# GpSimd's subtraction of a weight chunk in pieces of 256 columns, in a two-block transformer kernel

## The chip, the cores and the metric

The kernel runs on one core of one Trainium2 chip. The metric is the device time of one execution in microseconds (us). The engines are named as in the profile: PE is TensorE (PEld its weight loads), DVE is VectorE, ACT is ScalarE, POOL is GpSimd, SP is SyncE, which here only issues DMAs. An SP, ACT or POOL queue works strictly in order, and so does DVE's.

## The reference

Batch 1, 512 tokens, 1024 channels, all fp32. Two blocks follow each other. Cut to its big matrix products, the reference is:

```python
# first block, layer 0: gated MLP with a spatial unit, and a multiscale pool
h = x * (1 + scale) + shift                        # shift, scale, gate = silu(c) @ ada_w[l] + ada_b[l]
u, v, z_a, x_b, z_b = split(h @ e_w_in, 5)         # 1024 x 5120
a = u * (W_s @ layer_norm(v) + b) * silu(z_a)
b = (pool(x_b) @ pool_w + pool_b) * pool_scale * silu(z_b)
x = layer_norm(ALPHA * x + (1 + gate) * (concat(a, b) @ e_w_out))
# layer 1: latent attention, 16 heads
q_c, kv_c, k_r, z = split(h @ o_w_in); q = rms(q_c) @ w_uq; ...
x = layer_norm(ALPHA * x + (1 + gate) * ((attention * silu(z)) @ o_w_out))
# second block: short convolution, feed-forward, windowed attention, feed-forward
h = h + rmsnorm((b_gate * conv3(c_gate * u)) @ a_w_out)
h = h + rmsnorm((silu(g) * up) @ w_down)           # g, up = rmsnorm(h) @ w_gate_up, 1024 x 5632
h = h + rmsnorm(window_attention(...) @ b_w_o)
h = h + rmsnorm((silu(g) * up) @ w_down)
```

## The kernel before

**Split products.** Each fp32 operand of a large product is held as two tiles of a narrower fp32 format: a high part, which is a rounded copy, and a low part, which is the fp32 value minus the high part. A product is then three matmuls (`mm3`, lines 1589 to 1591): high by high, high by low, low by high.

**Weights.** All weights pass through a ring of two slots `s` = 0, 1. A chunk is 128 partitions by 2048 columns (`CHUNK`; 1280 for one slot of the latent attention). It goes through four stations: SP loads it into `w_raw[s]` (`load`, line 402); ACT copies it into `w_high[s]` (`split_high`, line 655); GpSimd forms `w_low[s]` = `w_raw[s]` - `w_high[s]` (`low`, line 589); PE reads high and low. The semaphores between them are `w_full`, `w_high`, `w_split` and `used`. When GpSimd is done, it frees `w_raw[s]` for the next load (`raw_free`). So with two slots, while PE works through one chunk of 48 matmuls of 512 columns, the other slot is freed by PE, copied by ACT and subtracted by GpSimd. A few chunks are split by DVE instead (`split_low`, line 1204), and the second chunk of the stages gu0, kv and gu1 is shared in halves (line 598 on GpSimd, 1212 on DVE).

**Stages**, in the order of the table `RING`: v, xb, zu, pool, zb, eout (layer 0), lat, mla (eight rounds of two heads), oout (layer 1), cu, b, aout (convolution), gu0, dn0 (feed-forward), kv, q, wo (windowed attention), gu1, dn1 (feed-forward).

**Other work on DVE.** DVE evacuates PSUM, does the normalisations, the softmax parts and the low parts of the activations. In stages xb, zu and zb it also multiplies and reduces the conditioning weights `ada_w`: two multiplications `gains<-gains,csil` of 1024 columns (line 1033, both inputs in SBUF) and two reductions to `ada_acc` (line 1036), whose results PE needs after each chunk (line 1636), and whose end lets SP load the next piece. The gated stages form `gate_buf` times PSUM (1159, 1163), times `sv` (1165), and the low part `mix_low` or `ff_low` (1168), the last two with both inputs in SBUF.

**Other work on GpSimd.** `pool_low` (line 626, 4096 columns, one instruction), eight passes over `x` by the layer norm's gain and bias (582, 584), and parts of the rotary of the windowed attention (571, 574). Every operation of an engine's program is in source order; there is no scheduler.

Of the kernel before, what the change touches and what calls it, by code (L numbers as in the profile page):

```python
# [6 lines left out]
F32 = mybir.dt.float32  # L7
F32R = mybir.dt.float32r
I32 = mybir.dt.int32
ALU = mybir.AluOpType  # L10
# [170 lines left out]


UNITS = KVH * T
CREDIT = 1


def program(nc, a, out):
    with ExitStack() as ctx:

        def sem(name):  # L190
            return ctx.enter_context(nc.semaphore(name))
# [6 lines left out]
        def at(name, offset, shape, dt=F32):  # L198
            return nc.alloc_sbuf_tensor_at(name, shape, dt, offset=start + offset)

        raw = [at(f"w_raw{s}", 8 * KB * s, [P, CHUNK]) for s in range(2)]
        WH = [at(f"w_high{s}", (16 + 8 * s) * KB, [P, CHUNK], F32R) for s in range(2)]
        WL = [at(f"w_low{s}", (32 + 8 * s) * KB, [P, CHUNK], F32R) for s in range(2)]
# [119 lines left out]
        w_split = [sem(f"w_split{s}") for s in range(2)]  # L323
# [37 lines left out]

        PF, n = {}, CREDIT
        for name in ("xb", "zu", "zb", "cu", "b", "gu0", "gu1"):
# [3 lines left out]
        SG, n = {}, 0  # L367
# [24 lines left out]
        def _(sp):  # L392
# [4 lines left out]
            def load(name, i, s, pieces):  # L397
                B = BASE[name]
                assert len(pieces) == B.dmas[s]
                sp.wait_ge(raw_free[s], B.use[s] + i + CREDIT)  # L400
                for dst, src in pieces:
                    sp.dma_start(dst, src).then_inc(w_full[s], 16)
# [9 lines left out]
            def deep(s, w, kt, n=2):  # L412
                c = n * D // 2
                return [(raw[s][:, j * c:(j + 1) * c], w[:, kt + j, :] if n == 2 else w[:, kt, j * c:(j + 1) * c]) for j in range(2)]
# [20 lines left out]
            def ada_load(layer, pos, first):  # L435

                for m in range(2):
                    sp.wait_ge(ada_sum[m], pos + CREDIT)
                    sp.dma_start(ada_buf[m], ada_w[layer][:, :, bass.ds(pos * 256 + (first + m * P), P)]).then_inc(ada_land[m], 16)
# [50 lines left out]
            for s in range(2):  # L490
                load("oout", 0, s, deep(s, w_in["o_w_out"], s * 2))
            sp.wait_ge(oz_ready, HEADS + CREDIT)
            for j, src in ((1, a["ln_g"][1:2, :]), (2, a["ln_b"][1:2, :]), (3, a["a_pre"])):
# [60 lines left out]
        @block.gpsimd  # L554
        def _(pool):
            nc.gpsimd.memset(eps[:, 0:1], LN_EPS)
            nc.gpsimd.memset(eps[:, 1:2], EPS2).then_inc(pool_ready, 1)
            for s in range(2):
                pool.sem_inc(raw_free[s], CREDIT)
                pool.sem_inc(pair_free[s], CREDIT)  # L560
            pool.sem_inc(gate_low, 2)
            pool.sem_inc(oz_ready, CREDIT)
            pool.sem_inc(sz_ready, CREDIT)
            for m in range(2):
                pool.sem_inc(ada_sum[m], CREDIT)

            def turn_queries(g):

                dst = q2[g % 2][:, :, :]
                pool.wait_ge(q2_raw, g + 1)  # L570
                nc.gpsimd.tensor_tensor(dst, q2raw[:, :, :], cosB.unsqueeze(1).broadcast_to((P, 2, S)), ALU.mult).then_inc(q2_cos, 1)
                pool.wait_ge(q2_cos, g)
                pool.wait_ge(q2_sin, g)
                nc.gpsimd.tensor_tensor(dst, dst, q2tmp[:, :, :], ALU.add).then_inc(q2_ready, 1)

            for name, pairs, _ in RING:
                B = BASE[name]
                if name == "mla":
                    pool.wait_ge(gains_in, 32)
                    for t in range(T):  # L580
                        pool.wait_ge(tr_done, T * TR["eout"] + t + 1)
                        nc.gpsimd.tensor_tensor(x[:, t, :], x[:, t, :], gains[:, 1, :], ALU.mult).then_inc(pool_step, 1)
                        pool.wait_ge(pool_step, t + 1)
                        nc.gpsimd.tensor_tensor(x[:, t, :], x[:, t, :], gains[:, 2, :], ALU.add).then_inc(x_ready, 1)

                def low(i, s, n=CHUNK):

                    pool.wait_ge(w_high[s], B.split[s] + i + 1)
                    nc.gpsimd.tensor_tensor(WL[s][:, 0:n], raw[s][:, 0:n], WH[s][:, 0:n].bitcast(F32), ALU.subtract).then_inc(w_split[s], 1)  # L589
                    pool.wait_ge(w_split[s], B.split[s] + i + 1)  # L590
                    pool.sem_inc(raw_free[s], 1)

                first, last = 0, pairs - (name in BOUNDARY)
                if name in SHARED:
                    low(0, 0)
                    pool.wait_ge(w_high[1], B.split[1] + 1)
                    h = CHUNK // 2
                    nc.gpsimd.tensor_tensor(WL[1][:, h:], raw[1][:, h:], WH[1][:, h:].bitcast(F32), ALU.subtract).then_inc(pool_half, 1)  # L598
                    pool.wait_ge(pool_half, SHARED.index(name) + 1)
                    pool.wait_ge(dve_half, SHARED.index(name) + 1)  # L600
                    pool.sem_inc(w_split[1], 1)
                    pool.sem_inc(raw_free[1], 1)
                    first = 1
                if name in SHARED and name in EARLY:
                    low(1, 1)
                    first = 2
                elif name in EARLY:
                    for s in range(2):
                        low(0, s, D if name in ("dn0", "dn1") else CHUNK)
                    low(1, 1)  # L610
                    first = 2
                if name == "q":
                    low(0, 0)
                    low(0, 1)
                    low(1, 0)
                    turn_queries(1)
                    low(1, 1)
                    turn_queries(2)
                    continue
                if name == "zu":  # L620
                    first = 2
                    for i in range(2):
                        for s in range(2):
                            low(i, s)
                    pool.wait_ge(pool_high, 1)
                    nc.gpsimd.tensor_tensor(poolL[:, :, :], pooled[:, :, :], poolH[:, :, :].bitcast(F32), ALU.subtract).then_inc(pool_low, 1)
                if name == "oout":
                    first = 1
                    low(0, 1)
                if name == "wo":  # L630
                    first = 1
                    low(0, 0)
                    turn_queries(3)
                    low(0, 1)
                if last > first:
                    with pool.Fori(first, last) as i:
                        for s in (1, 0) if name == "mla" else (0, 1):
                            low(i, s, MLA_CHUNK if name == "mla" and s else CHUNK)
                if name in BOUNDARY:
                    low(pairs - 1, 0)  # L640
# [3 lines left out]
        def _(act):  # L644
# [306 lines left out]
            def raw_queries(g):  # L951
                act.wait_ge(used[g % 2], BASE["q"].use[g % 2] + g // 2 + 1)
                if g == 1:
                    act.wait_ge(kd_ready, 1)
                act.wait_ge(q2_ready, g) if g else act.wait_ge(k2_rot, 1)
                nact(q2raw[:, :, :], PS[:, 0:2, :], ACT.Copy).then_inc(q2_raw, 1)

            def weigh2(n):

                w = 0 if n % T else P  # L960
                st, pr = soft[:, n % 2, :, :], p2[n % 3]
                act.wait_ge(m2_ready, n + 1)
                nact(st[:, 4, :], st[:, 3, :], ACT.Exp)
                for h in range(GROUP):
                    ins = nact(pr[:, h, w:], pr[:, h, w:], ACT.Exp, scale=SW_SCALE, bias=st[:, 2, h:h + 1], accum_out=st[:, 5, h:h + 1])
                ins.then_inc(e2_ready, 1)
# [16 lines left out]
            weigh2(0)  # L983
            for n in range(UNITS):
                g, b = n // T, n % T
                if b == 0 and g + 1 < KVH:
                    raw_queries(g + 1)
                if n + 1 < UNITS:
                    weigh2(n + 1)
# [12 lines left out]
        def _(dve):  # L1002
# [560 lines left out]
            top2(0)  # L1563
            for n2 in range(UNITS):
                g, b = n2 // T, n2 % T
                if n2 + 1 < UNITS:
                    top2(n2 + 1)
# [16 lines left out]
        def _(pe):  # L1584
# [468 lines left out]
            queries(1, 11, 2 * K)  # L2053
            for n in range(UNITS):
                g, b = n // T, n % T
                if n + 2 < UNITS:
                    score2(n + 2)
# [51 lines left out]
```

## Time and profile before

| | us |
|---|---|
| median of three runs | 2029.07 |
| lowest, highest | 2023.8, 2029.48 |
| span of the profiled execution | 2020.6 |
| PE busy | 1893.8 (94%) |
| DVE busy | 958.4 (47%) |
| ACT busy | 742.8 (37%) |
| POOL busy | 660.6 (33%), 603.3 of it in line 589 |

The profile is of one execution; its span leaves out some 8 us of start and end that the measured time has. PE's busy time counts matmuls whose ends are modelled, and it grows where the granted clock falls. The record of an instruction on DVE or POOL begins when the engine takes it up and not when it gets its data, so a record can hold a wait of which no semaphore tells.

### The profile page before, as it was taken

The numbers are of one execution on the slowest core, as the hardware profiler recorded it, in microseconds if no ns is written. First come the engines' busy times: TensorE is split into PE (matmuls) and PEld (weight loads), VectorE is DVE, ScalarE is ACT, GpSimd is POOL, SyncE is SP. The second block draws the span as 40 slices with busy tenths as digits, with TensorE's granted clock in tenths as the row PEclk, the third lists the DMA queues.
The fourth block names the chain that finished last, engine by engine and source line by source line (L and its number), as shares of the span: only waits on it lengthen the run. The fifth ranks groups of instructions, "written<-read, shape, count | busy, mean of one in ns | idle before, by whom it ended". The sixth has DMA issues, their size and how long they took to land.

```text
span 2020.6 us, 23910 instructions
## 1 busy us (share of the span) xinstructions
PE 1893.8 (94%) x9036; PEld 1546.9 (77%) x9036; DVE 958.4 (47%) x1273; ACT 742.8 (37%) x1024; POOL 660.6 (33%) x159
## 2 busy tenths in 40 slices
PE   5979889988999999979999999999989799999998
PEld 5768667876666666868888888888867688888887
DVE  6698888076454455075545223200667643222102
ACT  2213233154544445232225433421545444434312
POOL 1324444362211221323332434434233123434341
PEclk9989899999999999989999999999999899999999
DMA  8444544311121112323332333332221023333331
GB/s 289 125 119 131 139 131 172 104 57 34 34 67 34 34 54 95 105 63 84 125 104 78 89 104 93 106 124 90 92 84 42 22 84 86 101 104 94 103 103 64
DMA packets 227991, 190.04 MB, mean 94 GB/s; under 512 B 10727, under 2 KB 209498, under 8 KB 227930
## 3 DMA queue, kind: packets, MB, share of 16 engines
q1 hardware_dynamic: 227296, 188.91, 30.7%
q8 instruction: 42, 0.69, 0.1%
q10 hardware_dynamic: 634, 0.29, 0.1%
q14 instruction: 19, 0.16, 0.0%
HBM read 187.08 MB, written 2.10 MB: 94 GB/s over the span
## 4 chain that ended last, share of the span: by engine, by line
PE 65%; DVE 17%; issue 9%; ACT 5%; DMA 2%; SPq 1%; POOL 1%; DVEq 0%; ACTq 0%; POOLq 0%
PE PS L1589 20%; PE PS L1590 20%; PE PS L1591 20%; DVE gains L1033 2%; DVE ada_acc L1036 1%; DVE soft L1364 1%; ACT w_high L655 1%; PE PS L1700 1%; PE PS L2038 1%; SPq L426 1%; DMA w_raw<-in_e_w_in 1%; DMA ada_raw<-in_ada_w 1%; DVE probs L1371 1%; DVE q_rope L1346 1%; POOL w_low L598 1%
## 5 line engine op out<-in xcount | busy, mean ns | idle before, releaser
L589 POOL TENSOR_TENSOR w_low<-w_raw,w_high 128x2048 fp32r<-128x2048 f32 (+2 forms) x135 | 603.3, 4469 | 1273.6 <-ACT w_high L655 1273.6
L1589 PE MATMUL PS<-h_high,w_high 128*128 128x512 f32 (+1 forms) x1488 | 567.6, 381 | 14.3 <-DVE h_low L1272 5.5
L655 ACT ACTIVATE w_high<-w_raw 128x2048 fp32r<-128x2048 f32 (+1 forms) x150 | 281.9, 1879 | 763.0 <-PE PS L1591 659.2
L1590 PE MATMUL PS<-h_low,w_high 128*128 128x512 f32 (+1 forms) x1488 | 556.4, 374 | 0.0
L1591 PE MATMUL PS<-h_high,w_low 128*128 128x512 f32 (+1 forms) x1488 | 556.2, 374 | 0.0
L1589 PEld LDWEIGHTS PS<-h_high,w_high 128*128 128x128 f32 x1488 | 283.6, 191 | 76.1 <-issue 16.0
L1591 PEld LDWEIGHTS PS<-h_high,w_low 128*128 128x128 f32 x1488 | 283.5, 191 | 49.6
L1590 PEld LDWEIGHTS PS<-h_low,w_high 128*128 128x128 f32 x1488 | 283.9, 191 | 45.9 <-issue 0.5
L1204 DVE TENSOR_TENSOR w_low<-w_raw,w_high 128x2048 fp32r<-128x2048 f32 x12 | 27.5, 2292 | 351.5 <-ACT w_high L655 351.5
L1159 DVE TENSOR_TENSOR gate_buf<-gate_buf,PS 128x512 f32<-128x512 f32 x44 | 30.2, 687 | 280.2 <-ACT gate_buf L706 279.6
L1589 PE MATMUL PS<-w_high,ff_high 128*128 128x512 f32 x352 | 137.0, 389 | 0.0
L1591 PE MATMUL PS<-w_high,ff_low 128*128 128x512 f32 x352 | 136.9, 389 | 0.0
L1590 PE MATMUL PS<-w_low,ff_high 128*128 128x512 f32 x352 | 136.9, 389 | 0.0
L1168 DVE TENSOR_TENSOR ff_low<-gate_buf,ff_high 128x512 f32 x44 | 97.0, 2205 | 40.8 <-ACT ff_high L708 40.8
L1589 PE MATMUL PS<-w_high,o_high 128*128 128x512 f32 x192 | 75.0, 390 | 3.2 <-DVE o_low L1339 3.2
L1591 PEld LDWEIGHTS PS<-w_high,ff_low 128*128 128x128 f32 x352 | 66.1, 188 | 13.7
L1589 PEld LDWEIGHTS PS<-w_high,ff_high 128*128 128x128 f32 x352 | 66.1, 188 | 13.7
L1590 PEld LDWEIGHTS PS<-w_low,ff_high 128*128 128x128 f32 x352 | 66.1, 188 | 13.6
L1591 PE MATMUL PS<-w_high,o_low 128*128 128x512 f32 x192 | 74.7, 389 | 0.0
L1590 PE MATMUL PS<-w_low,o_high 128*128 128x512 f32 x192 | 74.7, 389 | 0.0
L831 ACT ACTIVATE probs<-PS,soft 128x128 f32<-128x128 f32 (+1 forms) x64 | 33.8, 528 | 108.7 <-DVE soft L1365 108.7
L1036 DVE TENSOR_REDUCE ada_acc<-gains 128x128 f32<-128x1024 f32 x32 | 62.2, 1983 | 0.0
(298 smaller groups left out, 2733.2 us busy)
## 6 DMA issues: line engine op xcount, KB each, us to landing
w_raw<-in_f_gate_up SPq DMA_DIRECT2D x88, 512.0 KB, 4.9
w_raw<-in_e_w_in SPq DMA_DIRECT2D x40, 512.0 KB, 6.1
w_raw<-in_f_down SPq DMA_DIRECT2D x40, 512.0 KB, 4.2
gains<-in_ada_w SPq DMA_DIRECT2D x32, 512.0 KB, 4.4
w_raw<-in_a_w_in SPq DMA_DIRECT2D x24, 512.0 KB, 4.2
w_raw<-in_o_w_in SPq DMA_DIRECT2D x20, 512.0 KB, 4.4
ada_raw<-in_ada_w SPq DMA_DIRECT2D x8, 1024.0 KB, 12.0
w_raw<-in_e_w_out SPq DMA_DIRECT2D x16, 512.0 KB, 4.3
```

What stands on the lines that cost most here:

```text
L426: sp.dma_start(ada_raw[c][:, :].rearrange("p (k n) -> p k n", n=256), ada_w[0][:, :, c * 256:(c + 1) * 256]).then_inc(ada_full[c], 16)
L589: nc.gpsimd.tensor_tensor(WL[s][:, 0:n], raw[s][:, 0:n], WH[s][:, 0:n].bitcast(F32), ALU.subtract).then_inc(w_split[s], 1)
L655: nact(WH[s][:, 0:n], raw[s][:, 0:n], ACT.Copy).then_inc(w_high[s], 1)
L831: nact(pm[u % 2][:, 0:w], PS[:, 2 + u % 2, 0:w], ACT.Exp, scale=MLA_SCALE, bias=soft[:, u % 2, 1, 0:1], accum_out=soft[:, u % 2, 2, 0:1]). ...
L1033: v.tensor_tensor(ada_buf[m], ada_buf[m], csil[:, :].unsqueeze(2).broadcast_to((P, K, P)), ALU.mult).then_inc(ada_prod[m], 1)
L1036: v.reduce_sum(ada_acc[m][:, :], ada_buf[m].rearrange("p k n -> p n k"), AX).then_inc(ada_sum[m], 1)
L1159: v.tensor_tensor(buf[s][:, :], buf[s][:, :], PS[:, 2 * s + 1, :], ALU.mult).then_inc(prod_ready, 1)
L1168: v.tensor_tensor(lows[:, f, :], buf[s][:, :], highs_of[name][:, f, :].bitcast(F32), ALU.subtract).then_inc(gate_low, 1)
L1204: v.tensor_tensor(WL[s][:, :], raw[s][:, :], WH[s][:, :].bitcast(F32), ALU.subtract).then_inc(w_split[s], 1)
L1589: mm(dst, lh, rh, start=first, stop=False, skip_group_check=True)
L1590: mm(dst, lh, rl, start=False, stop=False, skip_group_check=True)
L1591: return mm(dst, ll, rh, start=False, stop=last, skip_group_check=True)
```

## The change

GpSimd's subtraction of a chunk, one instruction over all `n` columns before, becomes a row of instructions over 256 columns each: eight for 2048 columns, five for 1280, four for 1024. Only the last one counts up `w_split`; nothing waits between the pieces. Nothing else changes: the halves of line 598, `pool_low` and the passes over `x` stay single instructions, as do DVE's own splits.

```diff
+SLICE = 256
 ...
                 def low(i, s, n=CHUNK):
 
                     pool.wait_ge(w_high[s], B.split[s] + i + 1)
-                    nc.gpsimd.tensor_tensor(WL[s][:, 0:n], raw[s][:, 0:n], WH[s][:, 0:n].bitcast(F32), ALU.subtract).then_inc(w_split[s], 1)
+                    for c in range(0, n, SLICE):
+                        piece = slice(c, c + SLICE)
+                        ins = nc.gpsimd.tensor_tensor(WL[s][:, piece], raw[s][:, piece], WH[s][:, piece].bitcast(F32), ALU.subtract)
+                    ins.then_inc(w_split[s], 1)
                     pool.wait_ge(w_split[s], B.split[s] + i + 1)
                     pool.sem_inc(raw_free[s], 1)
```

On GpSimd, around the first four chunks of stage zu and the first of the pool stage (`w_low_53` and `w_low_54` are the low tiles of slots 0 and 1), there stood before:

```order
L589 TENSOR_TENSOR w_low_53<-w_raw_49,w_high_51 128x2048
L589 TENSOR_TENSOR w_low_54<-w_raw_50,w_high_52 128x2048
L589 TENSOR_TENSOR w_low_53<-w_raw_49,w_high_51 128x2048
L589 TENSOR_TENSOR w_low_54<-w_raw_50,w_high_52 128x2048
L626 TENSOR_TENSOR pool_low<-pooled,pool_high 128x4096
```

and there stands now:

```order
L592 TENSOR_TENSOR w_low_53<-w_raw_49,w_high_51 128x256 x8
L592 TENSOR_TENSOR w_low_54<-w_raw_50,w_high_52 128x256 x8
L592 TENSOR_TENSOR w_low_53<-w_raw_49,w_high_51 128x256 x8
L592 TENSOR_TENSOR w_low_54<-w_raw_50,w_high_52 128x256 x8
L630 TENSOR_TENSOR pool_low<-pooled,pool_high 128x4096
```

No instruction changes place: each subtraction becomes eight at the same point of the row, and `pool_low` behind them stays whole. The other engines' rows are the same as before.

## Rows read from the trace of the kernel before

**Rows 1.** The page: its head and part 1

```profile
span 2020.6 us, 23910 instructions
PE 1893.8 (94%) x9036; PEld 1546.9 (77%) x9036; DVE 958.4 (47%) x1273; ACT 742.8 (37%) x1024; POOL 660.6 (33%) x159
```

**Rows 2.** Stretches: from:to, length, busy us, clock, DMA share, GB/s

```profile
100.00:335.00 235.00, 203.55 (x893) 168.42 (x892) 210.17 (x190) 67.18 (x64) 89.13 (x18) 0.93 0.47 139
...
425.00:480.00 55.00, 44.17 (x197) 36.19 (x196) 44.95 (x67) 31.71 (x64) 35.51 (x12) 0.88 0.23 63
...
870.00:910.00 40.00, 28.81 (x173) 26.51 (x173) 31.75 (x31) 16.34 (x25) 10.12 (x2) 0.83 0.20 53
...
1455.00:1605.00 150.00, 128.99 (x850) 102.51 (x850) 108.96 (x154) 76.99 (x193) 42.74 (x12) 0.94 0.15 50
```

**Rows 3.** Timeline in stage zu, POOL and DVE: start, us, engine, line, operation

```profile
195.08 9.25 POOL L626 TENSOR_TENSOR pool_low<-pooled,pool_high 128x4096 fp32r<-128x4096 f32 x1 [0.18 <-POOL w_low L589]
...
196.41 8.48 DVE L1168 TENSOR_TENSOR mix_low<-gate_buf,mix_high 128x512 f32 x1 [0.96 <-ACT mix_high L708]
...
204.30 4.99 POOL L589 TENSOR_TENSOR w_low<-w_raw,w_high 128x2048 fp32r<-128x2048 f32 x1
...
217.46 0.69 DVE L1168 TENSOR_TENSOR mix_low<-gate_buf,mix_high 128x512 f32 x1 [0.96 <-ACT mix_high L708]
```

**Rows 4.** Timeline, DVE in stage v and at the start of cu

```profile
49.00 3.23 DVE L1063 TENSOR_TENSOR h_low<-gains,h_high 128x1024 fp32r<-128x1024 f32 x1 [2.52 <-ACT h_high L681]
...
876.84 4.12 DVE L1280 SCALAR_TENSOR_TENSOR x_hat<-x,stat,gains 128x1024 f32<-128x1024 f32 x1
```

**Rows 5.** PE's waits: us in total, times, longest us

```profile
PE PS L1636 <- DVE ada_acc L1036: 11.0, 5, 6.4
...
PE PS L1589 <- DVE h_low L1063: 8.6, 6, 4.5
PE PS L1700 <- DVE x_hat L1280: 6.4, 2, 3.3
...
PE PS L1762 <- DVE mod L1041: 6.2, 1, 6.2
...
PE PS L1589 <- DVE sv L1178: 4.9, 1, 4.9
...
PE PS L1725 <- DVE mod L1041: 2.5, 1, 2.5
```

**Rows 6.** Timeline at the start of stage mla: three instructions in a row

```profile
435.76 2.70 POOL L584 TENSOR_TENSOR x<-x,gains 128x1024 f32<-128x1024 f32 x1
...
437.40 2.15 DVE L1250 SCALAR_TENSOR_TENSOR x<-x,hf 128x1024 f32<-128x1024 f32 x1
...
438.43 3.38 POOL L582 TENSOR_TENSOR x<-x,gains 128x1024 f32<-128x1024 f32 x1
```

**Rows 7.** POOL's groups by shape: line, names, shapes, count, busy, mean ns

```profile
L589 POOL TENSOR_TENSOR w_low<-w_raw,w_high 128x2048 fp32r<-128x2048 f32 x123 | 570.5, 4638 | 1060.7 <-ACT w_high L655 1060.7
L589 POOL TENSOR_TENSOR w_low<-w_raw,w_high 128x1280 fp32r<-128x1280 f32 x8 | 23.2, 2898 | 183.4 <-ACT w_high L655 183.4
...
L589 POOL TENSOR_TENSOR w_low<-w_raw,w_high 128x1024 fp32r<-128x1024 f32 x4 | 9.6, 2398 | 29.5 <-ACT w_high L655 29.5
```

**Rows 8.** Timeline of one round of mla: POOL, DVE, PE

```profile
510.68 4.59 POOL L589 TENSOR_TENSOR w_low<-w_raw,w_high 128x2048 fp32r<-128x2048 f32 x1 [6.80 <-ACT w_high L655]
...
514.12 1.70 DVE L1346 TENSOR_TENSOR q_rope<-q_raw,cos_m 128x512 f32<-128x512 f32 x1
...
517.18 0.47 PE L1589 MATMUL PS<-h_high,w_high 128*128 128x512 f32 x1 [0.30 <-PE PS L1591]
```

**Rows 9.** Timeline at the first lat chunk (POOL, PE) and in gu0 (POOL)

```profile
420.60 4.59 POOL L589 TENSOR_TENSOR w_low<-w_raw,w_high 128x2048 fp32r<-128x2048 f32 x1 [22.61 <-ACT w_high L655]
...
426.36 0.47 PE L1589 MATMUL PS<-w_high,h_high 128*128 128x448 f32 x1 [0.62 <-DVE h_low L1063]
...
1200.52 4.61 POOL L589 TENSOR_TENSOR w_low<-w_raw,w_high 128x2048 fp32r<-128x2048 f32 x1 [6.22 <-ACT w_high L655]
```

## The prediction

> **What bounds the kernel now.** I read the head of the page and part 1 first. PE is busy for 1893.8 of 2020.6 us [rows 1], so nothing that leaves PE's idle time as it is can gain much: some 127 us are to be had, and what a low clock costs. A busy time per stretch then says where they are [rows 2]. From 100 to 335 us (stages xb to zb) PE works 203.6 of 235 us and DVE shows 210.2, that is, DVE sets the pace. From 425 to 480 PE lacks 10.8 us, from 870 to 910 11.2, from 1455 to 1605 21.0. These four stretches hold 74.5 us of idle PE. They also hold the low clock: 0.93, 0.88, 0.83 and 0.94 of full speed [rows 2]. A mean of 0.93 over 235 us is about 33 us at the lower of two levels (1.2 instead of 2.4 GHz). PE loses at most half of such time, so 16.5, 6.6, 6.8 and 9 us, 39 in all.
>
> The third view is the timeline of DVE beside POOL. An operation of DVE with both inputs in SBUF and 512 columns takes 0.69 us; the same one, begun at 196.41, takes 8.48 us. POOL had begun `pool_low` at 195.08, and its record ends at 204.33; DVE's ends at 204.89, 0.56 us later [rows 3]. DVE stood behind GpSimd's instruction until it had ended. With twice the columns, 3.23 us at 49.00 and 4.12 at 876.84 show the same, against some 1.3 without a wait [rows 4], if the 0.69 is scaled. Since DVE works in order, all that is queued behind such an operation waits too, also reads of PSUM and the reductions. Last, the view of PE's waits: six rows that end on DVE hold 39.6 us: 11.0 on `ada_acc`, 8.6 on `h_low`, 6.4 on `x_hat`, 6.2 and 2.5 on `mod`, 4.9 on `sv` [rows 5].
>
> **What the change does to DVE's wait.** After it, an operation of DVE that comes while GpSimd subtracts should wait for one piece at most, if the data path changes hands between pieces. The nearest rows say that it does between two instructions of GpSimd in a row: line 584 ends at 438.46 and the next is taken up at 438.43, with no idle time between; yet DVE's operation, which waited since 437.40, ends at 439.55, inside the second, which then takes 3.38 us [rows 6]. The subtraction begun at 204.30 takes 4.99 instead of 4.62 for the same reason [rows 3, 7]. So DVE goes first at the border, and GpSimd's next instruction pays.
>
> The Trainium skill (SBUF — State Buffer, "Who interferes with whom") says the same as a rule: a DVE instruction with two SBUF inputs and a GpSimd instruction that reads SBUF exclude each other, for the whole instruction. By that rule alone a held operation would wait for 0 to 1 piece.
>
> **What a piece costs.** Columns of 2048, 1280 and 1024 take 4.64, 2.90 and 2.40 us [rows 7]. The slope between 1024 and 2048 is 2.19 ns a column, which leaves 0.16 us that do not scale; between 1280 and 1024 it is 1.95 ns, which leaves 0.40. A piece of 256 columns is then 0.56 + 0.16 = 0.72 or 0.50 + 0.40 = 0.90 us; with nothing fixed at all, 0.58. I take 0.75: the 2048 rows hold some contention themselves, so the true slope is a little lower. Eight pieces are 6.0 us (4.6 to 7.2), 1.4 more than now, and each operation of DVE that gets in between adds some 0.4 to 0.5.
>
> The Trainium skill (GPSIMD Engine Reference, "Performance pitfalls for Q7 kernels") gives some 102 cycles per read command that do not overlap with the one before. With two inputs and 1.2 GHz that is an estimate of 0.17 us a piece and 5.8 us for eight; the sum would differ by 0.2 us per chunk.
>
> **Where the longer subtraction is covered.** In the feed-forward stages, some 60 chunks, PE needs about 10.9 us a chunk: that is the cycle of POOL, 4.61 busy and 6.22 idle before [rows 9]. The slot must be copied by ACT (1.9 us, part of the idle time) and subtracted within it; 8.9 us are left for a subtraction of 6.0 to 7. That costs nothing, and it would cost from 1.1 us a piece on. It is not covered in two places. In each of eight rounds of mla the subtraction begins at 510.68 and PE takes the chunk up at 517.18, 6.5 us later; DVE's `q_rope` at 514.12 now gets in between [rows 8]. 6.0 + 0.5 just fits; at 0.90 a piece it is 1.2 us late, 10 us over eight rounds. I take 1 us for the eight. At the first chunk of lat the subtraction ends at 425.19 and PE begins at 426.36 [rows 9]; 6.0 us plus an operation of DVE makes that 1 us late. The first chunks of gu0, kv and gu1 have the same pattern, but there a later wait (for the half-chunk of line 598, unchanged) takes most of it up. 3 us for these four, so 4 in all.
>
> **What DVE gives back**, against the six rows of PE's waits [rows 5]. Each line is what I think goes, with the rest kept for the piece that is still waited for or for what is late next:
> - `ada_acc`, 11.0: 9. Behind the longest (6.4) stand the 8.48 us operation and the one after. In the new order GpSimd's chunk ahead of `pool_low` ends about 1.4 to 2 us later, and DVE's earlier operations go through sooner, so `mix_low` should pass before `pool_low` starts. One of the next two multiplications may be caught by `pool_low`, which stays whole; then half of the 6.4 comes back.
> - `h_low` line 1063, 8.6: 4, two waits of 2 us each [rows 4].
> - `x_hat`, 6.4: 5. The wait of 2.8 us at 876.84 goes but for a piece [rows 4], and one like it at the second pair of tiles.
> - `mod` before the spatial unit, 6.2: 3.5. Here DVE runs rows of additions with both inputs in SBUF; between two of them GpSimd now gets one piece each time, so DVE waits eight times for 0.6 us instead of once for 4. Only the multiplications and reductions behind them gain.
> - `sv`, 4.9: 3.5; `mod` before eout, 2.5: 2.5.
>
> That is 27.5 us. The block of windowed attention and the end of lat have smaller waits of the kind, and PE idles 21.0 and 10.8 us there [rows 2]; I take 8 for both. Of the 39 us that the low clock costs I take a quarter, 9: a fall follows an idle PE in these stretches, and only some of the idle time goes. I subtract 4 us for pieces that DVE now waits for where it met no subtraction before (the subtraction lasts a third longer). Sum: -27.5 - 8 - 9 + 4 + 4 = -36.5 us. On the profile's 2020.6 that is 1984; on the median of 2029.07 it is 1993. The two stand 8.5 us apart throughout, and the second is what is predicted.
>
> **Rivals.**
> 1. *The handover fails.* Between pieces nothing waits, whereas the pairs in rows 3 and 6 have a semaphore wait (already met) between them. If GpSimd keeps the data path over the row of eight, DVE waits for 6.0 instead of 4.6 us: 1.4 us more at some 16 places that PE waits for (22) and once in each of eight rounds of mla (11). I take a third of these 33 us as hidden and add the 4 of the longer subtraction: 26 more, 2055 us. It decides the sign by itself, from the first chunk on. The Trainium skill (GPSIMD Engine Reference, "Instruction dispatch") speaks for it: a core of GpSimd starts the next instruction as soon as its own share of the last is done, nothing holds it back. For the handover speak the two borders in the rows, neither with idle time on POOL. Chance 0.13.
> 2. *A piece costs more.* At 0.90 us mla loses 10 us, lat and its like 5, and DVE's waits grow by 2: 2005, still faster. At 1.05 mla loses 20, the others 8: 2020 to 2030, no change. Above 1.1 every chunk of the long stages is late, and the kernel is slower by tens of us. Against it: it needs 0.5 us fixed per instruction where the rows give 0.16 to 0.40. Chance 0.02 for the cheap end, 0.07 for about no change, 0.03 for slower.
> 3. *The clock comes back.* If all idle time behind DVE goes in a stretch, the low level goes with it. With 25 instead of 9 us for the clock, the time is 1977. Chance 0.12.
> 4. *The change does not do what it says*: DVE's waits go, but PE then waits for something else that was hidden (the loads of xb and zu are issued behind the reductions, `pool_low` and the passes over `x` still hold DVE). Half of the gain goes: 2011. Chance 0.13.
>
> **How the numbers follow.** Forecast as summed 0.50, rival 3 0.12, rival 4 0.13, rival 1 0.13, rival 2 0.12. Faster by over 0.3% (6 us, about what a measurement of this kernel can tell from no change): 0.50 + 0.12 + 0.13 + 0.02 = 0.77. Same: 0.07. Slower: 0.13 + 0.03 = 0.16. The likeliest case gives 1993 with its own range of 1980 to 2008. The range of 8 in 10 takes in rivals 3, 4 and the cheap half of 2: 1968 to 2022. Left out are rival 1, the slow part of rival 2 and 0.03 below.
>
> **What would show it.** In the profile after: POOL's groups by shape with 256 columns, at 0.65 to 0.80 us; DVE's operations of line 1168 in the feed-forward stages near 1.0 us mean; the rows of PE's waits on `ada_acc`, `x_hat` and `mod` much shorter; the clock of 100 to 335 us above 0.93. If DVE's operations still last until the eighth piece has ended, rival 1 holds. If PE waits for `w_low` in mla or the feed-forward stages, rival 2. The prediction is wrong if PE's idle time in the four stretches stays near 74 us.

## The result and the profile after

| | before | after |
|---|---|---|
| median, us | 2029.28 (4 runs) | 1996.02 (4 runs) |
| lowest, highest | 2023.8, 2030.85 | 1991.88, 1997.59 |
| ratio, 95% interval | | 0.9844, 0.9821 to 0.9867 |
| span of the profiled execution | 2020.6 | 1995.8 |

The change makes the kernel 1.6% faster. The forecast was 1993, its range 1968 to 2022.

One sentence ahead of the prediction was wrong: that a span leaves out some 8 us that the time has. Each execution's time is 1.8 us above its span (1997.59 against 1995.8 here). What stood between 2020.6 and the median of 2029 is that executions of the kernel before differ, 2020.4 to 2032.6 us in 19 runs, and the profiled one, 2022.38 us, was among the fastest. The traces below are compared with that one, so most show some 3 to 9 us less gain than the medians.

First the head of the page of the change's kernel and its first part: busy us of each engine, share of the span, number of instructions.

```profile
span 1995.8 us, 24815 instructions
...
PE 1887.3 (95%) x9036; PEld 1542.7 (77%) x9036; DVE 799.6 (40%) x1273; ACT 742.8 (37%) x1024; POOL 871.0 (44%) x1064
```

Against [rows 1], DVE does the same 1273 instructions in 158.8 us less, and POOL works 210.4 us more. The work of DVE has not changed, so at least 159 us of its busy time had been waiting. PE's busy time falls by 6.5 us and its idle time in all from 126.8 to 108.5, by 18.3; together they are the 24.8 us by which the span is shorter.

The same four stretches as in [rows 2]. The kernel now comes to the same work earlier, so each stretch here begins and ends at the matmuls that began and ended it before (from:to, length, busy us of PE, PEld, DVE, ACT, POOL, clock, DMA share, GB/s):

```profile
98.44:318.39 219.95, 197.90 (x892) 163.93 (x891) 170.16 (x186) 66.57 (x63) 126.47 (x137) 0.96 0.50 148
408.74:462.81 54.07, 40.74 (x197) 33.33 (x195) 45.32 (x66) 31.77 (x63) 41.67 (x31) 0.94 0.13 35
851.16:891.54 40.38, 30.04 (x173) 27.91 (x172) 26.77 (x30) 16.51 (x25) 18.73 (x16) 0.81 0.19 53
1437.64:1579.87 142.23, 127.67 (x851) 101.90 (x850) 98.54 (x154) 76.61 (x193) 54.01 (x54) 0.94 0.16 53
```

PE's idle time in them falls from 74.5 to 60.3 us: by 9.4 in the first and 6.4 in the last, while it grows by 2.5 in the second and hardly changes in the third. The clock rises in the first two, from 0.93 to 0.96 and from 0.88 to 0.94. The first stretch is 15.1 us shorter and the last 7.8. PE's waits (total, times, longest), to be held against [rows 5]:

```profile
PE PS L1593 <- POOL w_low L592: 25.4, 12, 5.3
...
PE PS L1824 <- DVE latent_norm L1319: 7.1, 1, 7.1
...
PE PS L1593 <- DVE h_low L1067: 4.4, 5, 2.1
...
PE PS L1766 <- DVE mod L1045: 1.0, 1, 1.0
PE PS L1704 <- DVE x_hat L1284: 0.9, 1, 0.9
...
PE PS L1729 <- DVE mod L1045: 0.3, 1, 0.3
```

`ada_acc` (11.0 before) is gone, `x_hat` has 0.9 of 6.4, the two rows of `mod` 1.0 of 6.2 and 0.3 of 2.5, `h_low` of the former line 1063 4.4 of 8.6. But a new row stands at the head: 25.4 us for `w_low`, GpSimd's subtraction itself, which had 0.3 before. Where DVE had been late because of GpSimd, it is now GpSimd's chunk that is late.

What the pieces do for one operation of DVE is seen at `sum_a`, in the kernel before:

```profile
125.33 4.62 POOL L589 TENSOR_TENSOR w_low<-w_raw,w_high 128x2048 fp32r<-128x2048 f32 x1 [18.19 <-ACT w_high L655]
125.76 4.73 DVE L1137 TENSOR_TENSOR sum_a<-xbuf 128x512 f32<-128x512 f32 x1 [0.77 <-ACT xbuf L717]
```

and in the change's:

```profile
127.65 6.70 POOL L592 TENSOR_TENSOR w_low<-w_raw,w_high 128x256 fp32r<-128x256 f32 x8 [2.26 <-ACT w_high L659]
...
131.73 0.87 DVE L1141 TENSOR_TENSOR sum_a<-xbuf 128x512 f32<-128x512 f32 x1
```

It begins in the middle of eight pieces and takes 0.87 instead of 4.73 us: at the border of a piece the data path goes to DVE, though GpSimd waits for no semaphore there. The eight pieces take 6.70 us, with it and the next two sums let in.

The new wait, in stage zu, where [rows 3] stood:

```profile
186.00 9.80 POOL L630 TENSOR_TENSOR pool_low<-pooled,pool_high 128x4096 fp32r<-128x4096 f32 x1 [0.18 <-POOL w_low L592]
195.76 8.42 POOL L592 TENSOR_TENSOR w_low<-w_raw,w_high 128x256 fp32r<-128x256 f32 x8
...
197.32 0.88 DVE L1172 TENSOR_TENSOR mix_low<-gate_buf,mix_high 128x512 f32 x1 [0.97 <-ACT mix_high L712]
...
204.31 0.79 PE L1593 MATMUL PS<-h_high,w_high 128*128 128x512 f32 x1 [5.29 <-POOL w_low L592]
```

`mix_low` takes 0.88 instead of 8.48 us. But four operations of DVE (`gate_buf`, `mix_low` and two multiplications of 1024 columns) get in between the pieces of the chunk behind `pool_low`. The chunk takes 8.42 us instead of 4.99, and PE waits 5.29 for it.

### The profile page after: what moved, and what is told of

It is laid out like the page before. It is cut to its first block, busy times and chain, and to the rows that moved or that the text cites. A ratio compares the mean times of both kernels' runs of the same rounds, so it can differ in the third digit from the quotient of the medians.

```text
span 1995.8 us, 24815 instructions
## 1 busy us (share of the span) xinstructions
PE 1887.3 (95%) x9036; PEld 1542.7 (77%) x9036; DVE 799.6 (40%) x1273; ACT 742.8 (37%) x1024; POOL 871.0 (44%) x1064
## 4 chain that ended last, share of the span: by engine, by line
PE 72%; DVE 10%; issue 8%; ACT 4%; POOL 3%; DMA 2%; SPq 1%; DVEq 0%; ACTq 0%; POOLq 0%
PE PS L1593 22%; PE PS L1595 22%; PE PS L1594 22%; POOL w_low L592 3%; PE PS L1901 2%; DMA w_raw<-in_e_w_in 1%; ACT w_high L659 1%; DVE soft L1368 1%; DVE ada_acc L1040 1%; PE PS L1704 1%; SPq L427 1%; PE PS L2042 1%; DVE gains L1037 1%; DMA ada_raw<-in_ada_w 1%; PE PS L1894 1%
## 5 line engine op out<-in xcount | busy, mean ns | idle before, releaser
L592 POOL TENSOR_TENSOR w_low<-w_raw,w_high 128x256 fp32r<-128x256 f32 x1040 | 815.0, 820 | 1051.8 <-ACT w_high L659 1051.7
L1595 PEld LDWEIGHTS PS<-w_high,ff_low 128*128 128x128 f32 x352 | 66.1, 188 | 13.7
L1172 DVE TENSOR_TENSOR ff_low<-gate_buf,ff_high 128x512 f32 x44 | 41.3, 938 | 40.8 <-ACT ff_high L712 40.8
```

The costliest lines, as they stand in the source:

```text
L592: ins = nc.gpsimd.tensor_tensor(WL[s][:, piece], raw[s][:, piece], WH[s][:, piece].bitcast(F32), ALU.subtract)
L1172: v.tensor_tensor(lows[:, f, :], buf[s][:, :], highs_of[name][:, f, :].bitcast(F32), ALU.subtract).then_inc(gate_low, 1)
L1595: return mm(dst, ll, rh, start=False, stop=last, skip_group_check=True)
```

## The experiments

To see where time is won, the start of the k-th matmul on PE in each trace is subtracted from that of the same matmul in the kernel before (there are 9036 in all of them). The table holds the gain up to the given time of the kernel before; "mla" is 475 to 747 us, the windowed attention block lies between 1461 and 1604.

| us gained up to | 99 | 335 | 475 | 747 | 908 | 1461 | 1604 | 2012 | medians |
|---|---|---|---|---|---|---|---|---|---|
| the change (256) | 1.7 | 16.6 | 16.8 | 21.6 | 19.3 | 17.4 | 25.2 | 24.8 | 33.3 |
| 1024, with surplus | -1.7 | 5.0 | 4.6 | -4.7 | -2.5 | -2.5 | 5.6 | 5.6 | 8.3 |
| 1024, exact | 0.1 | 7.2 | 7.3 | 9.3 | 9.7 | 9.7 | 17.0 | 17.0 | 23.9 |
| 512 | 1.9 | 19.1 | 19.1 | 21.1 | 24.5 | 24.5 | 30.9 | 30.9 | 36.5 |
| 128 | -0.7 | -1.2 | -4.0 | -6.1 | -10.2 | -13.7 | -3.7 | -5.0 | -2.1 |
| 256, all of GpSimd | 1.5 | 14.0 | 13.3 | 18.7 | 19.7 | 15.3 | 24.6 | 23.1 | 23.0 |
| 256, in mla only | -2.8 | -0.8 | -1.3 | 3.4 | 2.1 | 2.1 | 2.4 | 2.4 | 10.2 |
| 256, not early | -2.0 | 3.6 | -0.7 | 3.9 | 5.1 | 3.2 | 11.2 | 10.9 | 17.9 |
| 256, early only | 1.7 | 15.2 | 16.3 | 16.6 | 14.3 | 12.9 | 14.1 | 14.1 | 16.9 |
| 512, mla 256 | 2.3 | 20.2 | 21.9 | 26.7 | 32.7 | 32.7 | 37.7 | 37.7 | 44.5 |
| 512, all, mla 256 | 2.0 | 17.0 | 21.0 | 25.7 | 30.3 | 28.5 | 36.5 | 36.4 | 40.5 |
| before, once more | -1.8 | 1.1 | -0.5 | -0.2 | -1.8 | -3.3 | -2.3 | -2.3 | |

**Theory:** DVE waits for one piece instead of one chunk; each piece adds a fixed price to GpSimd, and each operation of DVE that is let in adds its own time. What a size is worth is the balance of the two. Rivals: the gain is the clock's; it comes from one stage; finer is always better. The first four runs change the size.

**Pieces of 512.** (Here and with 1024 a chunk of 1280 columns is cut at whole pieces, so 256 or 768 columns too many are subtracted.)

```
-SLICE = 256
+SLICE = 512
```

> Four pieces of 512 columns. Theory 1: a piece of 1.25 us; a chunk of 5.0 us alone against 5.6 with 256, and at most three or four DVE operations in between, so PE's waits on w_low (25.4 us with 256 columns) fall to 10 us or less, while DVE's waits grow by some 0.3 us each: 1990 to 1999 us, about the same as with 256. Rival (finer is better all the way down): 2001 to 2006 us.

Measured: 1991.11 us, ratio 0.9823 (0.9794 to 0.9852). As expected, and 5 us below the change, though the two intervals overlap. The rival, 2001 to 2006 us, falls. In the traces PE waits 7.8 us for `w_low` where it waits 25.4 with 256.

**Pieces of 1024.**

```
-SLICE = 256
+SLICE = 1024
```

> GpSimd's subtraction of a chunk in two pieces of 1024 columns instead of eight of 256. Theory 1 (DVE waits for the piece in progress, and the chunk gets longer by the fixed part of each piece and by every DVE operation let in between): a held operation still waits for up to 2.4 us, the chunk lasts 4.6 to 4.8 us alone, so PE's waits on w_low nearly go, but only about half of the gain is left: 2008 to 2016 us. Rival (the gain comes with any border between instructions, the length does not matter): 1993 to 1998 us.

Measured: 2019.35 us, ratio 0.9964 (0.9949 to 0.998). Less gain than expected, and the table shows a loss of 9.3 us in mla. The rival, that any border will do, falls too.

**Pieces of 128.**

```
-SLICE = 256
+SLICE = 128
```

> Sixteen pieces of 128 columns. Theory 1: a piece of 0.43 to 0.47 us from record to record (0.70 with 256 columns, of which 0.16 to 0.2 are fixed), a chunk of 7.2 us alone and up to 14 us where DVE has two-input operations all the time; each round of mla is some 0.8 us later, xb to zb and oout lose more: 2008 to 2022 us. Rival (finer is better all the way down, because DVE waits less): under 1994 us.

Measured: 2029.72 us, ratio 1.0018 (0.9999 to 1.0037): no difference to the kernel before, so finer is not always better. I had the cost too low. DVE gains still (782.6 us busy, 17.0 less than with 256), but all of it is given back. PE's waits for `w_low` say where: first the row of 512, then that of 128; with 256 it is 25.4.

```profile
PE PS L1593 <- POOL w_low L592: 7.8, 7, 2.0
```

```profile
PE PS L1593 <- POOL w_low L592: 58.0, 29, 8.0
```

The price of a piece can be read in the feed-forward stages, where little disturbs it. One chunk each of the kernels with whole chunks, pieces of 1024 (exact), 512, 256 and 128:

```profile
1113.48 4.61 POOL L589 TENSOR_TENSOR w_low<-w_raw,w_high 128x2048 fp32r<-128x2048 f32 x1 [6.16 <-ACT w_high L655]
```

```profile
1103.79 4.75 POOL L592 TENSOR_TENSOR w_low<-w_raw,w_high 128x1024 fp32r<-128x1024 f32 x2 [5.57 <-ACT w_high L659]
```

```profile
1099.97 5.49 POOL L592 TENSOR_TENSOR w_low<-w_raw,w_high 128x512 fp32r<-128x512 f32 x4 [5.45 <-ACT w_high L659]
```

```profile
1095.68 6.06 POOL L592 TENSOR_TENSOR w_low<-w_raw,w_high 128x256 fp32r<-128x256 f32 x8 [4.65 <-ACT w_high L659]
...
1099.15 1.30 DVE L1172 TENSOR_TENSOR ff_low<-gate_buf,ff_high 128x512 f32 x1 [0.92 <-ACT ff_high L712]
```

```profile
1113.32 7.27 POOL L592 TENSOR_TENSOR w_low<-w_raw,w_high 128x128 fp32r<-128x128 f32 x16 [22.21 <-ACT w_high L659]
```

The last three hold one operation of DVE each. Without one (the lower quartile of the 123 chunks of 2048 columns, from first start to last end) they take 4.60, 4.74, 5.02, 5.60 and 6.74 us: 0.14 us for each further instruction, whatever its size. The 38 chunks in which just one `ff_low` of 512 columns is let in have medians of 5.49, 6.12 and 7.25, so it adds 0.5. Where DVE is dense, many are let in: the longest 5% of the change's chunks take over 8.3 us.

**All of GpSimd's instructions in 256.** The passes over `x` ahead of mla, the half-chunks and `pool_low` too:

```
-nc.gpsimd.tensor_tensor(x[:, t, :], x[:, t, :], gains[:, 1, :], ALU.mult).then_inc(pool_step, 1)
+for c in range(0, D, SLICE):
+    p = slice(c, c + SLICE)
+    ins = nc.gpsimd.tensor_tensor(x[:, t, p], x[:, t, p], gains[:, 1, p], ALU.mult)
+ins.then_inc(pool_step, 1)
```

(and so for the addition, for `WL[1][:, h:]` and for `poolL`)

> As the changed kernel, and also pool_low (4096 columns), the eight passes over x (1024 columns) and the three half-chunks in pieces of 256. Theory 1: DVE's eight diag operations at the start of mla, which wait for a whole pass each (8.6 us for six), shorten to some 4 us, worth up to 5 us; pool_low lets DVE's gate_buf through (3.3 us) but ends 2 us later, which the subtraction behind it pays; the half-chunks are late by 0.4 us each: 1990 to 1996 us in all. Rival (these instructions lie beside other work): 1995 to 1999 us.

Measured: 2004.57 us, ratio 0.989 (0.9864 to 0.9916). A miss: 8.5 us slower than the change by the medians; its trace, of the fastest of its four runs, is 1.7 us behind. PE's row for `w_low` grows once more:

```profile
PE PS L1606 <- POOL w_low L598: 38.3, 12, 10.4
```

The 10.4 stand behind `pool_low`, which takes 15.76 instead of 9.80 us, and 7.2 more behind the passes over `x`.

**Pieces of 1024, exact.** Was the loss in mla that of the surplus columns?

```
-SLICE = 256
+SLICE = 1024
-                        piece = slice(c, c + SLICE)
+                        piece = slice(c, min(n, c + SLICE))
```

> The same pieces of 1024 columns, but the chunks of 1280 columns (the second chunk of each of mla's 8 rounds) end at their last column. In pieces_of_1024 a chunk of 1280 was done as 1024 + 1024, so 768 columns too many, about 1.7 us a round at 4.64 us for 2048. Matmul by matmul that kernel lost 9.3 us between 475 and 747 us of the kernel before, 1.2 a round. Theory A (those surplus columns hold mla's chain, probs on DVE or the chunk itself): the loss goes, 2008 to 2013. Theory B (DVE is held for a piece of 1024 at a worse moment than for one of 2048, surplus or not): it stays at 2017 to 2021, with PE's wait for probs L1375 still at some 12 us.

Measured: 2005.53 us, ratio 0.9891 (0.9869 to 0.9914). Theory A, 2.5 us below its range: mla now gains 2.0 us where it lost 9.3. So 768 surplus columns a round cost 11 us over the eight rounds. `probs` stands behind them: PE's wait for it is 12.9 us with the surplus and 4.8 without (6.3 in the kernel before). The two kernels at the same place, with the surplus and in the kernel before (0.49 is what 512 columns take undisturbed):

```profile
500.98 2.34 DVE L1375 TENSOR_SCALAR probs<-probs,soft 128x512 f32<-128x512 f32 x1
```

```profile
502.80 1.29 DVE L1371 TENSOR_SCALAR probs<-probs,soft 128x384 f32<-128x384 f32 x1
504.20 0.49 DVE L1371 TENSOR_SCALAR probs<-probs,soft 128x512 f32<-128x512 f32 x1
```

**Pieces of 256 in mla only.**

```
-                    for c in range(0, n, SLICE):
-                        piece = slice(c, c + SLICE)
+                    width = SLICE if name == "mla" else n
+                    for c in range(0, n, width):
+                        piece = slice(c, c + width)
```

> Pieces of 256 in the 8 rounds of mla alone, whole chunks elsewhere. My prediction priced mla at a loss of 1 us; the change's trace shows its rounds at 39.0 instead of 39.7 us. Theory A (the gain of a round is its own: probs and q_rope on DVE are no longer held behind a whole chunk): 4 to 5.5 us faster than before, 2022 to 2024. Theory B (mla's rounds were shorter only because the stages ahead handed over earlier): no difference, 2026 to 2029.

Measured: 2019.3 us, ratio 0.9951 (0.9933 to 0.997). Theory B falls. In the trace 4.7 us are gained between 475 and 747, as theory A has it, and none elsewhere. The median says 10.2 (6 to 14), more than theory A. Some 7 us of it is how far the profiled execution of before lies below its median; why pieces in mla alone should win those too was not found. In the round, the 384 columns of `probs` that took 1.29 now take 0.51:

```profile
502.21 3.83 POOL L593 TENSOR_TENSOR w_low<-w_raw,w_high 128x256 fp32r<-128x256 f32 x5 [23.57 <-ACT w_high L660]
...
504.02 0.51 DVE L1376 TENSOR_SCALAR probs<-probs,soft 128x384 f32<-128x384 f32 x1
...
511.47 6.10 POOL L593 TENSOR_TENSOR w_low<-w_raw,w_high 128x256 fp32r<-128x256 f32 x8 [5.43 <-ACT w_high L660]
```

and the chunk of [rows 8] ends at 517.57, 0.40 ahead of the matmul that takes it:

```profile
517.97 0.47 PE L1594 MATMUL PS<-h_high,w_high 128*128 128x512 f32 x1 [0.30 <-PE PS L1596]
```

**Pieces of 256 everywhere but early** (whole chunks in v, xb, zu, pool, zb).

```
+                    width = SLICE if name not in ("v", "xb", "zu", "pool", "zb") else n
```

> Whole chunks in v, xb, zu, pool and zb (up to 335 us), pieces of 256 in all stages behind. Matmul by matmul the change had gained 16.6 of its 24.8 us by 335 us. Theory A (parts add up): this kernel keeps the other 8, so 2018 to 2021. Theory B (the stages behind profit because they start from a DVE that has caught up; alone they give less): 2023 or more. Theory C (late handover into the later stages gives them more to win): 2012 or less.

Measured: 2011.53 us, ratio 0.9927 (0.9904 to 0.9951). By the median that is in theory C's range, but I had worked the numbers out from the trace, where 10.9 us are gained and 8 were expected. Of the 10.9, 3.6 stand in the table at 335 us, and the first chunk in pieces begins only at 327.75, so most of them are no work of the pieces. The other half decides.

**Pieces of 256 early only**, the other half.

```
+                    width = SLICE if name in ("v", "xb", "zu", "pool", "zb") else n
```

> Pieces of 256 only in v, xb, zu, pool and zb, whole chunks behind: the other half of pieces_of_256_not_early, which took 18 us off the median of 2029.5. Theory A (the halves add up to the change's 33): 15 us off, 2012 to 2017. Theory B (a gain ahead is lost again behind, because the next stage is then bound by a whole chunk holding DVE): under 9 us off, 2020 or more. Theory C (each half wins part of the same waits): both halves are worth more alone than together, 2009 or less.

Measured: 2010.34 us, ratio 0.9917 (0.9891 to 0.9943). That lies between theory A and theory C. The halves add up as far as this can be told: 10.9 + 14.1 = 25.0 in the traces, where the whole change has 24.8, and 17.9 + 16.9 = 34.8 in the medians, where it has 33.3. So close an agreement is partly luck, since each of the three medians has an interval of about 5 us to either side, and a trace wanders by some 3 us. The rival that one stage holds all of the gain falls, and theory B of both runs too. Theory C is not shown; an overlap of a few us is left open.

**Pieces of 512, and 256 in mla.**

```
+                    width = 256 if name == "mla" else 512
```

> Pieces of 512 everywhere, 256 in mla (where 1280 is a whole number of them). In mla (475 to 747 us) pieces of 256 had gained 4.8 us and pieces of 512 2.0; everywhere else 512 was as good or better (28.9 against 20.0 us in all). Theory A (a fixed price for each piece against a shorter hold of DVE, stage by stage): the gains add to 28.9 + 4.8 = 33.7, less than 1 us of it lost at the seams, so 1986 to 1990, and PE's wait for w_low stays near 8 us. Theory B (the two sizes differ by where the trace happened to land): 1991 to 1996.

Measured: 1984.96 us (1984.09 to 1986.2), ratio 0.9787 (0.9765 to 0.981). Theory A, a little better than it said: the traces give 37.7 us where 33.7 were added up. It is the fastest kernel of the study, 11 us below the change, and the two intervals lie apart. Since the two have the same pieces in mla, this shows that 512 beats 256 outside mla. Against pieces of 512 throughout, the trace gains 6.8 us more, of which 2.8 lie in mla, where alone the two differ; the intervals overlap. And there 256 also ends the chunk of 1280 at its last column, where 512 subtracted 256 columns too many. Which of the two gave the 2.8 was not tested. PE's wait for `w_low` is at the 7 us of 512:

```profile
PE PS L1594 <- POOL w_low L593: 7.0, 8, 1.6
```

**All of GpSimd's instructions in 512, mla's chunks in 256.** The edit is that of all in 256, with the two widths of the last kernel.

> Pieces of 512, 256 in mla's chunks, and now also the two passes over x ahead of mla (8 instructions of 1024 columns), the halves of a chunk, and pool_low (4096 columns in 8 pieces). In pieces of 256 the same addition lost 8.5 us against the change. Theory A (that loss was the price of the many pieces: 32 passes of 0.84 us made mla's first chunk 7 us late, and the long pool_low the chunk behind it): here the price is some 1.5 us of GpSimd for pool_low and 2 us for the passes, PE's wait of 4.4 for latent_norm goes, and the time is 1981 to 1986. Theory B (these four instructions are better left whole at any size, since GpSimd is what is late there): 1988 to 1993.

Measured: 1986.66 us, ratio 0.9805 (0.9787 to 0.9823). Between the two theories, and no gain over leaving those instructions whole (1984.96). PE's wait for `latent_norm`, which theory A let go, stays: 4.9 us against 4.4. Of `pool_low`:

```profile
187.79 12.69 POOL L643 TENSOR_TENSOR pool_low<-pooled,pool_high 128x512 fp32r<-128x512 f32 x8 [0.18 <-POOL w_low L599]
...
207.48 0.79 PE L1607 MATMUL PS<-h_high,w_high 128*128 128x512 f32 x1 [8.30 <-POOL w_low L599]
```

`pool_low` takes 12.69 us instead of 9.81, and PE waits 8.30 for the chunk behind it, where it waits less than 0.9 with `pool_low` whole. By 335 us, before which `pool_low` is all that differs, the kernel has gained 17.0 instead of 20.2; with 256 it is 14.0 instead of 16.6. As one instruction `pool_low` holds DVE longer, but PE needs the chunk behind it first.

**The kernel before, once more.** No edit.

> The kernel before, unchanged, for a second profiled execution. The profiled one had a span of 2020.6 us, while most executions of this kernel have a span of 2027 to 2028 at a granted clock 0.002 lower; pieces in mla alone took 10 us off the median, but only 2.4 us off the profiled execution. Theory A (executions differ by how TensorE's clock falls, in the stretches where it is below 1 anyway: 100 to 335, 425 to 480, 1455 to 1605): PE's clock is lower there, and no round of mla differs. Theory B (they differ in mla, where DVE's held operations come in another order): the rounds are longer, 40.5 us or more instead of 39.7. If the execution is again one near 2020, the question stays open.

Measured: 2024.65 us. The rounds of mla are the same to 0.3 us in all (table), so theory B falls. The losses come in steps. Two stretches of the first trace and of the second:

```profile
0.00:100.00 100.00, 77.44 (x348) 66.55 (x349) 68.64 (x150) 24.82 (x32) 28.68 (x12) 1.00 0.64 209
...
790.00:870.00 80.00, 80.00 (x354) 66.23 (x354) 21.88 (x26) 23.86 (x29) 27.59 (x6) 1.00 0.39 125
```

```profile
0.00:100.00 100.00, 76.95 (x338) 65.82 (x339) 66.97 (x148) 24.70 (x31) 28.68 (x12) 0.98 0.64 209
...
790.00:870.00 80.00, 80.00 (x347) 66.02 (x346) 20.27 (x23) 22.79 (x26) 27.58 (x6) 0.98 0.38 125
```

The clock (the third figure from the end) is 0.98 instead of 1.00 in both, and some 1.7 us are lost in each. So the two executions do differ by the clock, but not where theory A put it: these are stretches where it had been 1.00, while from 100 to 335 us it is 0.94 against 0.93, and 2.9 us are gained. This execution's span is only 2.3 us above the first, not 7, so one at the median was not seen. It shows how much a trace may wander by itself: up to some 3 us in one stretch. The change's 2.8 lost between 789 and 876 and 1.9 between 908 and 1461 are of this size and kind, and I read nothing into them.

## Why the prediction was right, and where it was not

- **The handover at a piece's border** (rival 1 against it): right. `sum_a` 0.87 instead of 4.73, `mix_low` 0.88 instead of 8.48, line 1172 in the feed-forward stages 938 ns on average, where 1.0 us was named. The Trainium skill (SBUF — State Buffer, "Who interferes with whom") says that the two engines exclude each other for a whole instruction; the trace agrees, with a piece as the instruction: these operations wait for 0.2 us instead of 4 and 7.8.
- **The price of a piece:** right. By the medians 0.74 us in the record and 0.70 from start to start, 0.75 said; eight pieces 5.60, 6.0 said; one operation let in 0.5, 0.4 to 0.5 said. The mean of the group is 820 ns, above the 0.65 to 0.80 that was to be seen, because a piece's record also holds the operation of DVE let in before it.
- **Covered in the feed-forward stages:** right for 256. Of the 123 chunks of 2048 columns, in all stages, only one (10.63 us, at 866.36) took over the 8.9 us named as the limit, and none of PE's waits for `w_low` lies in the feed-forward stages.
- **mla:** wrong in sign, and the kernel with pieces in mla alone shows it. "I take 1 us for the eight" lost; 4.7 were gained. The step looked at the chunk's handover alone [rows 8], which fits by 0.40 us as worked out, and not at what the other chunk of the round, of 1280 columns, holds on DVE. `probs` was in none of the rows I read.
- **Not covered "in two places":** this is the step that failed. At the first chunk of lat, one of the places named, PE waits 1.6 us for `w_low`, about as said. But the price of the longer subtraction was sought only where PE took a chunk up right behind it in the old trace. It came where DVE had been held: there many operations are let in. Five of PE's new waits, 18.4 of 25.4 us, stand behind chunks that take 7.4 to 10.6 us instead of 6; by place, 18.2 of the 25.4 lie between 100 and 335 us, which the sum put at nothing. The waits were 1.3, 7.8, 25.4 and 58.0 us with pieces of 1024 (exact), 512, 256 and 128, so they follow the number of pieces.
- **What DVE gives back:** `ada_acc` 11.0 (9 said), `x_hat` 5.5 (5), the `mod` rows 5.2 and 2.2 (3.5 and 2.5; 1.5 us of the first is a new wait for `sv` at the same matmul), `h_low` 4.2 (4), `sv` 4.9 (3.5), nearly all at least what was said. But the time gained up to 335 us, 16.6, is less than the 18 to 20 of these terms that lie there. And at the second block's start the 5.5 of `x_hat` came to 0.4 (18.9 at 876 to 19.3 at 908), since PE now waits 3.76 for `w_low` there; with pieces of 512, which cut that wait, the same stretch gains 5.9. Rival 4 was thus partly true beside the forecast: the held operations went, and the next thing hidden was GpSimd's own chunk, which that rival did not name.
- **Lat's end, part of the 8:** wrong. 5.2 us are lost between 450 and 463. All kernels that cut the chunks of eout and lat to 512 or less but leave the passes over `x` whole lose there (2.0 to 6.0); "early only", "mla only" and 1024 lose nothing. With the passes cut too, all in 256 gains 2.8 here, but PE then waits 7.2 for the first chunk of mla, and all in 512 still loses 1.8. DVE's `diag` meets more of the unsliced passes over `x`: before, the last pass ended 4.7 us after the first `diag` there began, now 9.5. The kernel before, then the change's:

```profile
451.63 5.80 DVE L1047 TENSOR_SCALAR diag<-small,mod 128x128 f32<-128x128 f32 x8
```

```profile
431.13 3.38 POOL L583 TENSOR_TENSOR x<-x,gains 128x1024 f32<-128x1024 f32 x1
...
432.31 10.96 DVE L1051 TENSOR_SCALAR diag<-small,mod 128x128 f32<-128x128 f32 x8
```

  10.96 instead of 5.80 us, and PE's 7.1 us for `latent_norm` (2.6 before) stand behind it. **Windowed attention**, the other part, gave 7.8 (17.4 to 25.2), and gives 5 to 10 in every kernel that cuts chunks there.
- **The clock:** 9 said. Over the whole span it is granted at 0.983 instead of 0.980. By the prediction's own measure that is at most (0.020 x 2020.6) - (0.017 x 1995.8) = 6.5 us, and PE's busy time falls by as much. The rival that all of the gain is the clock's falls with that, and rival 3, with 25 us for the clock, too.
- **The sum:** -36.5 said, -24.8 from trace to trace, -33.3 from median to median. The forecast came out 3 us low on the median. The terms, though, were all read from traces, and against the trace the sum was 12 too good: the new waits for `w_low` are 25.4 us where 4 were taken, mla gave 5.7 more than its forecast, and the rest is spread. That the median hit better is luck: the profiled execution of before lay 7 us under the median of its four runs, and the change's 1.6 over its own; the prediction took the first distance for a constant of the measurement.

## What to carry to other kernels

When GpSimd holds a data path that DVE needs, cut its instruction into the largest pieces at which nobody waits long, not the smallest: here 512 beat 256 outside mla, 128 won nothing, and 1024 won two thirds of what 512 did by the medians. Choose the size by stage: large or whole where the next thing needed is GpSimd's own output (`pool_low`), smaller where a short operation of DVE is on PE's path in every round (mla; there whole chunks lost 4.7 us to 256, and whether 256 is better than an exact 512 is open). End the last piece at the last column: surplus columns cost 11 us in mla. And price the longer instruction in the places where the other engine had been held, because that is where its cuts are used.

## What the runs showed that I had not expected

- An instruction of GpSimd costs 0.14 us that do not scale, the same at 1024, 512, 256 and 128 columns. The Trainium skill (GPSIMD Engine Reference, "Performance pitfalls for Q7 kernels") led to 0.17 a piece; the trace is near it, and the measured 0.14 decides.
- DVE's `TENSOR_SCALAR` with one tensor input is held too: `probs` of 384 columns took 1.29 instead of 0.51 us. `diag` of 128 columns takes 0.27 alone; the last of the first eight took 4.62 us with whole chunks, and 2.43, 1.33, 0.76 and 0.48 with pieces of 1024, 512, 256 and 128.
- An operation of 512 columns let in costs GpSimd 0.5 us, for 0.69 of DVE's record when it is alone, so no price of the handover itself shows.
- A stretch with PE busy throughout may run at a clock of 0.98 in one execution and 1.00 in the next of the same kernel, and cost 1.6 us.
